# Six held weight pieces instead of four in a two-block transformer kernel, with a smaller scratch for dynamic DMAs

## What is computed

```python
q = (xb @ wq).reshape(t, HEADS, 2, DQ // 2)
s = einsum('thpd,hpkd->thpk', q, subkeys)
s_top, i_top = lax.top_k(s, 16)                  # for both halves of the key
cand = s_top[:, :, 0, :, None] + s_top[:, :, 1, None, :]
c_top, c_idx = lax.top_k(cand, 16)
e = i1 * 128 + i2;  g = softmax(c_top)
act = gelu(einsum('thkd,td->thk', u[e], xb))
out = einsum('thk,thkd->td', g * act, v[e])
```

## Time and profile before

| | |
|---|---|
| median of three executions | 2077.7 us (2076.5 to 2079.97) |
| the profiled execution, its own time | 2080.77 us |
| its span in the trace | 2078.6 us |
| PE busy | 1730.2 us (83%), 7686 matmuls |
| DVE, ACT, POOL busy | 1340.5, 924.7, 859.3 us |
| moved by DMA | 637.15 MB, 307 GB/s over the span |
| first block's gathers | issued from 173.6 us on |
| second block's gathers | issued from 1411.6 us on |

### The profile page before, as it was taken

The page is one execution under the profiler, slowest core; times in us unless marked ns, Lnnn a source line. Parts: engine busy times, 40 slices in busy tenths (PEclk is TensorE's granted clock), DMA queues, the critical chain, the costliest instruction groups (busy, mean ns, idle before and its releaser), DMA issues.

```text
span 2078.6 us, 22827 instructions
## 1 busy us (share of the span) xinstructions
PE 1730.2 (83%) x7686; PEld 1069.4 (51%) x7686; DVE 1340.5 (64%) x2906; ACT 924.7 (44%) x2363; POOL 859.3 (41%) x778
## 2 busy tenths in 40 slices
PE   8987988877877777887889898887889878777786
PEld 7985444322322222787889898884444322222222
DVE  4668667766766654598535675348677667667654
ACT  5554554444444443544124334454544444444443
POOL 3335333333333332576355436544333333333331
PEclk9999999999999999999999999999999999999999
DMA  6447999999999999343013233448999999999996
GB/s 227 136 158 307 421 420 420 421 422 421 421 422 421 421 421 385 98 137 112 21 41 102 82 102 122 151 165 360 420 421 421 422 421 421 422 421 422 421 422 290
DMA packets 102052, 637.15 MB, mean 307 GB/s; under 512 B 11264, under 2 KB 12544, under 8 KB 36272
## 3 DMA queue, kind: packets, MB, share of 16 engines
q0 software_dynamic: 75216, 543.27, 62.9%
q1 hardware_dynamic: 26720, 92.43, 13.9%
HBM read 634.61 MB, written 1.05 MB: 306 GB/s over the span
## 4 chain that ended last, share of the span: by engine, by line
PE 38%; DMA 37%; DVE 13%; ACT 7%; issue 3%; POOL 1%; SPq 0%; DVEq 0%; ACTq 0%; POOLq 0%
DMA arena<-in_uv,arena 30%; PE pb L587 15%; DMA spare<-in_uv,arena 6%; PE pb L336 5%; PE pb L337 4%; PE pb L338 4%; DVE arena L1555 3%; ACT arena L1004 3%; PE pb L409 1%; PE pb L700 1%; POOL parts L1991 1%; PE pb L714 1%; PE pb L709 1%; PE pb L792 1%; ACT arena L999 1%
## 5 line engine op out<-in xcount | busy, mean ns | idle before, releaser
L587 PE MATMUL pb<-arena 128*128 128x512 f32 x1848 | 916.5, 626 | 224.9 <-ACT arena L1004 223.9
L1555 DVE SCALAR_TENSOR_TENSOR arena<-arena,pb 128x1024 f32<-128x1024 f32 x462 | 563.4, 1220 | 372.7 <-DMA arena<-in_uv,arena 372.6
L2013 POOL DMA_INDIRECT arena<-in_uv,arena x462 | 440.3, 953 | 721.2 <-PE pb L587 701.1
L587 PEld LDWEIGHTS pb<-arena 128*128 128x128 f32 x1848 | 325.2, 193 | 782.0 <-ACT arena L1004 515.2
L1991 POOL TENSOR_TENSOR parts<-ring,parts 128x512 fp32r<-128x512 f32 x228 | 335.0, 1485 | 360.2 <-ACT parts L847 339.0
L996 ACT ACTIVATE arena<-arena 128x1 f32<-128x1 f32 x512 | 103.2, 202 | 616.4 <-DVE arena L1555 556.8
L847 ACT ACTIVATE parts<-ring 128x512 fp32r<-128x512 f32 x328 | 201.5, 627 | 255.6 <-PE pb L338 252.8
L336 PE MATMUL pb<-xl,parts 128*128 128x256 f32 x704 | 223.6, 318 | 9.3 <-DVE xl L1249 5.9
L1004 ACT ACTIVATE arena<-cst,arena 128x128 f32<-128x128 f32 x512 | 205.5, 401 | 47.2 <-ACT arena L999 0.4
L336 PE MATMUL pb<-parts,xh 128*128 128x256 f32 x608 | 179.9, 296 | 28.1 <-POOL parts L1991 17.6
L337 PE MATMUL pb<-xh,parts 128*128 128x256 f32 x704 | 202.4, 287 | 0.0
(11 more groups left out here) (287 smaller groups left out, 1810.3 us busy)
## 6 DMA issues: line engine op xcount, KB each, us to landing
ring<-in_w_in SPq DMA_DIRECT2D x108, 512.0 KB, 3.5
ring<-in_wq SPq DMA_DIRECT2D x32, 512.0 KB, 4.4
ring<-in_w_out SPq DMA_DIRECT2D x16, 512.0 KB, 4.0
arena<-in_uv,arena POOLq DMA_INDIRECT x462, 20.2
ring<-in_wa SPq DMA_DIRECT2D x8, 512.0 KB, 3.6
ring<-in_wb SPq DMA_DIRECT2D x8, 512.0 KB, 3.5
arena<-in_sk POOLq DMA_DIRECT2D x2, 1024.0 KB, 6.2
arena<-in_tail POOLq DMA_DIRECT2D x1, 1280.0 KB, 9.6
```

Of the source, the lines that this page charges most:

```text
L587: ins = pe.matmul(ys[hf][:, :], diags[:, k % 4, :], lands[k % LANDS][:, D + hf * 512:D + (hf + 1) * 512], start=k % (8 * K) == 0, stop=k % ...
L1555: ve.scalar_tensor_tensor(z, z, 1.0, xg[t], ALU.mult, ALU.mult, accum_out=hidden[:, k:k + 1]).then_inc(*up("v_dot", ("dot", e, k)))
L2013: gp.indirect_dma_start(lands[k % LANDS], None, rows_uv, bass.IndirectOffsetOnAxis(ap=eidx[:, k:k + 1], axis=0)).then_inc(*up(f"dma_rows{k ...
```

## The change

PARTS is 6 instead of 4, so `parts` has 24 KB in a partition where it had 16 KB, and the program object is given `dynamic_dma_scratch_size=8192`, where the default is 16384. Nothing else is changed in the text; by PARTS, the lead of every `ahead`, the slot of a piece, the piece whose use ACT waits for and POOL's `ahead(8 * 4 - PARTS - 8)` and `ahead(PARTS)` in the expert layer follow.

```diff
@@ -19,7 +19,7 @@
 SLOTS = 4
-PARTS = 4
+PARTS = 6
 LANDS = 10
@@ -2145,7 +2145,7 @@
-    nc = bacc.Bacc("TRN2", target_bir_lowering=False, num_devices=1)
+    nc = bacc.Bacc("TRN2", target_bir_lowering=False, num_devices=1, dynamic_dma_scratch_size=8192)
```

## The result

The changed kernel takes **2084.06 us** in the median of 20 executions (2079.91 to 2094.26), the kernel before 2080.1 in the median of 20. The ratio is **1.0028**, with an interval from 1.0017 to 1.0039: slower by 3.5 to 8.1 us. The ratio goes by the means of all executions, which the long ones of the changed kernel raise; the medians differ by 4.0 us. A second set of 12 executions gave 1.0018 (1.0007 to 1.0030). My forecast was 2.6 us slower, 2080.3 us. It counted from the median of three executions, 2077.7, so its distance to 2084.06 is not all the change: 2.4 us of it lie in the kernel before.

What follows compares the result with a forecast made beforehand. It took full DMA queues to bound the gathers and TensorE to lead elsewhere. Later gathers and start (2 x 6.0, +1.4), less earlier blocks (2 x 1.25) and shorter waits, gave +2.6 on 2077.7: 2080.3 us, range 2072.5 to 2089.

Steps and rivals of the forecast that it cites:

- step 1: First gather of both expert layers: VectorE's call now waits for q12 and q13, so each comes 6.0 us later.
- step 2: One weight block of 0.524 MB moves ahead of the first gather in each layer: -1.25 us each, bounds 0 and 1.25.
- step 3: Kernel start: ScalarE makes six pieces before the second group of features, +1.4 us, between +0.7 and +2.6.
- 70.07: TensorE's 2.38 us wait for a POOL low part goes; a bank freed by VectorE limits the gain to -1.0 us.
- step 4: TensorE's waits for pieces shrink, from 70.07 us through block two's last residual; two pieces are worth 2.9 us; 8.3 us in all.
- 1161: TensorE's largest wait, 5.56 us at 1161.07, shrinks by two pieces, -2.9 us, limited by POOL's pace.
- faster* rival: Two pieces carry TensorE over its waits, so the clock isn't lowered: -7.4, 2070.3 us; needs faster POOL splits at 1161; chance 0.17.
- 871.53: TensorE's wait for a piece there shrinks: -0.7 us, between 0 and 0.97, as VectorE's convolution runs at about the same pace.
- The head norm: VectorE's split and the norm behind it come two pieces earlier: -1.5 us, between 0 and -2.9.
- The last residual: End of block two: only q2 and q3 are split before it, their high parts two pieces earlier: -1.3 us.
- the gains don't reach the end: Rival: each removed stall returns as a wait for VectorE; late gathers, start and bytes remain: +10.9, 2088.6 us; chance 0.28.
- The scratch: Rival: POOL waits for room to write gather descriptors in the smaller DMA scratch, 2130 us or more; chance 0.05.

Runs made afterwards that it cites:

- the chain edit: POOL splits an item's pieces behind the next three groups' masks in the chain of L700; against the kernel before: four pieces 2069.9 us (0.9947), six 2075.97 us (0.9972).
- the second execution of the changed kernel: The changed kernel run again unaltered for a second profile: median 2083.41 us over 12 executions; the profiled one took 2085.07 us.
- all four edits: Six pieces, VectorE's position moved by 6, POOL's loads first, four pieces at the start, POOL's splits behind the masks: 2061.78 us, ratio 0.9910 to the kernel before.
- the kernel with POOL's loads first: Six pieces, but POOL splits q4 and q5 only behind its three expert-layer loads: 2092.38 us, ratio 1.0059 to the kernel before.

## Why the prediction was right or wrong

The direction was right, the time within the range, and the size half of the measured one (2.6 against 5.8, or 5.2 with the chain quiet); 2.6 lies just below the interval of the first comparison, 3.5 to 8.1. The terms are best compared in the two kernels with the chain edit, whose spans are 2065.8 (four pieces) and 2073.6 (six). ScalarE's roots and table loads (L868) stand at the ends of stages; four pieces first:

```profile
158.45 0.20 ACT L868 ACTIVATE small<-small 128x2 f32<-128x2 f32 x1 [1.27 <-DVE small L1229]
537.87 1.28 ACT L868 ACT_TABLE_LOAD   x1
843.95 0.20 ACT L868 ACTIVATE small<-small 128x2 f32<-128x2 f32 x1 [0.23 <-DVE small L1229]
1381.45 1.28 ACT L868 ACT_TABLE_LOAD   x1
1757.08 1.28 ACT L868 ACT_TABLE_LOAD   x1
```

```profile
158.88 0.20 ACT L868 ACTIVATE small<-small 128x2 f32<-128x2 f32 x1 [1.27 <-DVE small L1229]
543.90 1.28 ACT L868 ACT_TABLE_LOAD   x1
849.79 0.20 ACT L868 ACTIVATE small<-small 128x2 f32<-128x2 f32 x1 [0.23 <-DVE small L1229]
1385.08 1.28 ACT L868 ACT_TABLE_LOAD   x1
1765.16 1.28 ACT L868 ACT_TABLE_LOAD   x1
```

The lead of the four-piece kernel is 0.4 us at the first row scale, 6.0 in the middle of the first gathers, 5.8 at their end, 3.6 at the second row scale and 8.1 behind the second first gather. By terms:

| term | predicted | measured |
|---|---|---|
| start and the wait at 70, up to the first row scale | +0.4 | +0.4 |
| first gathers, behind the row scale | +6.0, +6.0 | +7.2, +5.3 |
| one block less behind them | -1.25, -1.25 | -1.6, -0.9 |
| block two, between the gather phases | -7.3 | -2.2 |
| sum | +2.6 | +8.2 |

The measured column is one pair of executions. Their spans differ by 7.8 us, the medians of the two kernels by 6.1 and the ratios by 5.2, so some 2 us of the column belong to this pair. The +0.4 in the first line is such a case: in the pair of the kernel before and the changed kernel the lead at the first row scale is 1.8 us (158.08 and 159.90).

**The late gathers (step 1): right, and the mechanism exactly so.** DVE's two splits stand where they were foretold, against the end of item 1. In the changed kernel q13's high part is written at 171.60, and the first gather follows 10.94 us later; the prediction had 11.06. From L1481 to the gather it is 8.35 us, predicted 8.4. The second layer is 0.7 us under its term. The first is 1.2 over it, and that has a cause of its own that I missed: POOL, too, was moved past something. Its longer lead brings q4 and q5 in front of its three loads. I had counted this as a gain (POOL done before the experts' choice) and not looked at what was queued behind: TensorE waits 2.10 us for the keys where it had waited 0.78 for the query. Putting the loads back takes 1.33 and 1.36 us off the distance.

**One block less (step 2): right.** After the first gather SP issues five loads of `wq` by 264 us where it issued six, and the lead shrinks by 1.6 and 0.9 us.

**The start (step 3) and 70.07: right in sum by luck, not in parts.** The table load at 18.35 comes 1.3 us later in the changed kernel, as predicted, but TensorE's wait grew by 1.86 us. At 70.07 the 2.38 us wait and the low clock behind it did go; the wait for the bank that replaced it came with a low clock of its own (0.81 between 75 and 80 us). The changed kernel was 2.92 us behind at 25 us and is 2.90 behind at 88: nothing in place of -1.0, and 2.9 in place of 1.4 for the start, more than its bound of 2.6. What brought the sum nearer again came later, at the end of the stage, where a wait of 1.89 us for a low part of DVE's at 110.54 had gone, which I had no term for.

**Block two (step 4): the term that failed.** -2.9 at 1161 was right: from the root in front to the products behind, the lead of the four-piece kernel fell from 7.15 to 4.20 us. In between TensorE of the six-piece kernel was 1.6 us ahead of the four-piece kernel, and POOL's pace took that back in waits of 3.32, 0.41 and 1.58 us; this is the condition on which the *faster* rival hung, and it isn't met. The first wait for a piece at this place, and the waits for L1661 and L1938, four pieces and then six:

```profile
896.03 2.08 PE L632 MATMUL pb<-arena,cst 128*128 128x512 f32 x2 [4.79 <-DVE arena L1661]
...
1148.15 0.56 PE L336 MATMUL pb<-parts,xh 128*128 128x256 f32 x1 [5.41 <-POOL parts L1991]
...
1250.01 2.02 PE L802 MATMUL pb<-arena 128*128 128x128 f32 x16 [2.24 <-DVE arena L1938]
```

```profile
901.96 2.08 PE L632 MATMUL pb<-arena,cst 128*128 128x512 f32 x2 [7.50 <-DVE arena L1661]
...
1155.22 0.53 PE L336 MATMUL pb<-parts,xh 128*128 128x256 f32 x1 [3.32 <-POOL parts L1991]
...
1253.69 3.21 PE L802 MATMUL pb<-arena 128*128 128x128 f32 x16 [3.38 <-DVE arena L1938]
```

What failed:
- 871.53: the 0.97 us and the slow clock behind it went, then the wait for L1661 was 7.50 instead of 4.79 us: 0 in place of -0.7.
- At 950 something was added that I had not looked at. TensorE waited 2.57 us for a copy of ScalarE (L858) instead of 1.61, and the clock, which had stayed up before, fell; the low parts gained behind it (five waits) ended in the 9.34 us wait for L1738. +1.2 us by the root ahead of 1161.
- The wait for L1938 grew from 2.24 to 3.38 us, and here too the clock fell where it had stayed up before: +1.1 us, where I had -0.9 for the small waits in front of it. This is in part chance: in the second execution of the changed kernel the clock stayed up behind the same wait, and the stage between the two table loads took 121.3 us, against 123.4 here and 124.8 with four pieces.
- The head norm: ScalarE's root came 2.3 us earlier against the products, as foretold, and a wait of 3.03 us for POOL's low part went, but the wait for DVE's grew from 1.42 to 3.92 us. -1.1 in place of -1.5. The last residual gave between 0.5 (this pair) and 1.4 us (the first pair of traces), predicted 1.3.

The wait for ScalarE's copy in TensorE's timeline, and the stretch around it, four pieces and then six:

```profile
947.70 2.46 PE L647 MATMUL pb<-cst,arena 128*128 128x128 f32 x20 [1.61 <-ACT arena L858]
```

```profile
947.00:952.00 5.00, 4.30 (x37) 4.23 (x38) 5.00 (x8) 3.89 (x9) 4.13 (x3) 1.00 0.35 105
```

```profile
953.60 4.07 PE L647 MATMUL pb<-cst,arena 128*128 128x128 f32 x20 [2.57 <-ACT arena L858]
```

```profile
953.00:958.00 5.00, 4.40 (x25) 4.38 (x26) 3.78 (x7) 3.58 (x8) 3.99 (x3) 0.66 0.32 105
```

So the rival *the gains don't reach the end* described this half of the kernel better than the forecast did. It was not all of it either: 2.2 of 7.3 us arrived, and by the figures of L1938 some 2 us more would have with the clock up there (an estimate). With all four edits 2.9 us arrive in block two.

**The scratch:** the rival was rightly small. **Slower by over 0.2%** had 0.42, *same* 0.43: the measured 0.28% lies on the far side of a bound that the forecast itself nearly touched.

What stays open is why the chain's clock fell at all three waits in one profiled execution of the changed kernel and at none in the other, in what share of executions of either kernel it does so, and why all six executions of the kernel with POOL's loads first were long. The long times could have been read as the price of that edit, had the edit not been tried without the waits.

## What to carry to other kernels

When a lead or a buffer count grows, list for every engine what its call now stands in front of, the DMA issues among it: the same two pieces were worth 8 us or cost 5 us, by where a few calls and loads stood. A wait taken off TensorE usually comes back as the next wait, grown, and it can take back all that it gave if the clock falls there: at 70.07 nothing was left of 2.38 us. Where executions of one kernel differ by more than the change, find the wait behind which they part and remove it in both kernels; then measure the change.

## What the runs showed of the hardware

TensorE's clock fell to the lower of its two levels behind one and the same wait of 3.28 us in one execution and not in another, and each fall cost 2.2 us in this chain. The wait of some 3.4 us for L1938 (3.35 to 3.41) was followed by a fall in seven of the ten traces with six pieces. It fell behind the wait of 2.57 us for L858 in all ten (granted clock 0.66 over 5 us in the one shown), and behind the wait of 2.21 us for L1407 in nine (0.81 between 75 and 80 us in the changed kernel). In the three traces with four pieces it stayed up behind the wait of 1.6 us for L858 and that of 2.24 us for L1938. Which waits are followed by a fall can't be told from their length alone. With the three waits of the chain the 20 executions of the changed kernel spread over 14 us, without them the seven over 3.4.

A DMA scratch of 8192 bytes instead of 16384 left the median gather issue at 937 ns and the time as it was (ratio 1.0006, 0.9998 to 1.0015).
